# Projecting queries and keys with one 512-column matmul for both halves of the input, in a three-block transformer kernel on one core

## What is computed

```python
# layer 0 of attention (odd_mixer): 16 heads of 64
z = h @ w_in                       # queries, keys, values, and 8 forget gates
y_c = forgetting_attention(...)    # heads 0 to 7, "fox"
y_d = moba_attention(...)          # heads 8 to 15, with a relative bias, "moba"
# layer 1 of attention (second_block)
proj = xn @ w_in                   # queries, keys, values of both kinds
sb_out = stick_breaking_attention(...)      # 8 heads, "stick"
diff_out = differential_attention(...)      # 4 heads with two maps each, "diff"
```

## Time and profile before

| | us |
|---|---|
| median of three executions | 933.09 |
| the profiled execution, its own time | 936.74 |
| its span, first to last instruction | 935.0 |
| TensorE busy in the span | 916.9 |
| VectorE busy | 667.6 |
| ScalarE busy | 552.3 |
| attention steps, layer 0 | about 288 to 379 |
| attention steps, layer 1 | about 594 to 690 |

### The profile page before, as it was taken

The page is one execution under the profiler, slowest core; times in us unless marked ns, Lnnn a source line. Parts: engine busy times, 40 slices in busy tenths (PEclk is TensorE's granted clock), DMA queues, the critical chain, the costliest instruction groups (busy, mean ns, idle before and its releaser), DMA issues.

```text
span 935.0 us, 19813 instructions
## 1 busy us (share of the span) xinstructions
PE 916.9 (98%) x6898; PEld 865.6 (93%) x6898; DVE 667.6 (71%) x1296; ACT 552.3 (59%) x938; POOL 173.5 (19%) x94
## 2 busy tenths in 40 slices
PE   8999999999999999999999999999999999999996
PEld 7999888889998999988888999989999999999996
DVE  6886887786547665788778755787468877785566
ACT  7356776664435556576676545466557666664453
POOL 2320544420000002044443000000203444410000
PEclk9999999999999999999999999999999999999998
DMA  7557765567533544466556653444335655566521
GB/s 276 173 178 218 241 203 184 190 213 263 168 135 106 165 137 136 138 223 204 193 186 213 218 177 135 137 158 136 117 104 186 198 184 180 189 216 205 176 92 46
DMA packets 46329, 163.51 MB, mean 175 GB/s; under 512 B 5010, under 2 KB 9618, under 8 KB 46277
## 3 DMA queue, kind: packets, MB, share of 16 engines
q1 hardware_dynamic: 41704, 158.19, 51.4%
q10 hardware_dynamic: 4573, 4.62, 1.8%
HBM read 161.71 MB, written 3.44 MB: 177 GB/s over the span
## 4 chain that ended last, share of the span: by engine, by line
PE 84%; DVE 6%; issue 5%; ACT 2%; DMA 1%; POOL 1%; SPq 0%; DVEq 0%; ACTq 0%; POOLq 0%
PE psum L1349 17%; PE psum L1370 17%; PE psum L1371 16%; PE psum L1372 16%; PE psum L1350 8%; DVE wl L872 2%; PE psum L1481 1%; PE psum L1483 1%; PE psum L1484 1%; PE psum L1591 1%; DMA raw<-in_even_in 1%; PE psum L1566 1%; ACT wh L534 1%; PE psum L1554 1%; ACT work L712 0%
## 5 line engine op out<-in xcount | busy, mean ns | idle before, releaser
L534 ACT ACTIVATE wh<-raw 128x1024 fp32r<-128x1024 f32 (+2 forms) x270 | 301.1, 1118 | 166.3 <-PE psum L1372 155.0
L872 DVE TENSOR_TENSOR wl<-raw,wh 128x1024 fp32r<-128x1024 f32 (+2 forms) x204 | 272.3, 1339 | 83.7 <-ACT wh L534 83.2
L475 POOL TENSOR_TENSOR wl<-raw,wh 128x1024 fp32r<-128x1024 f32 x66 | 160.0, 2425 | 620.6 <-ACT wh L534 620.6
L1349 PE MATMUL psum<-xs,wh 128*128 128x512 f32 x704 | 247.1, 397 | 0.3 <-POOL wl L475 0.3
L1370 PE MATMUL psum<-xs,wh 128*128 128x256 f32 x800 | 229.7, 287 | 4.3 <-DVE wl L872 2.6
L1371 PE MATMUL psum<-xs,wh 128*128 128x256 f32 x800 | 226.2, 283 | 0.0
L1372 PE MATMUL psum<-xs,wl 128*128 128x256 f32 x800 | 226.2, 283 | 0.0
L1350 PE MATMUL psum<-xs,wl 128*128 128x256 f32 x704 | 196.4, 279 | 0.0
L1370 PE MATMUL psum<-ys,wh 128*128 128x256 f32 x672 | 190.9, 284 | 0.1
L1371 PE MATMUL psum<-ys,wh 128*128 128x256 f32 x672 | 190.1, 283 | 0.0
L1372 PE MATMUL psum<-ys,wl 128*128 128x256 f32 x672 | 190.1, 283 | 0.0
(11 more groups left out here) (212 smaller groups left out, 1008.7 us busy)
## 6 DMA issues: line engine op xcount, KB each, us to landing
raw<-in_up SPq DMA_DIRECT2D x132, 512.0 KB, 3.3
raw<-in_down SPq DMA_DIRECT2D x48, 704.0 KB, 4.3
raw<-in_qkv SPq DMA_DIRECT2D x48, 512.0 KB, 3.3
raw<-in_even_in SPq DMA_DIRECT2D x16, 512.0 KB, 4.0
raw<-in_out SPq DMA_DIRECT2D x16, 512.0 KB, 3.4
raw<-in_ple SPq DMA_DIRECT2D x8, 640.0 KB, 3.9
raw<-in_even_out SPq DMA_DIRECT2D x8, 512.0 KB, 3.3
toeplitz_dram<-table_dram ACTq DMA_DIRECT2D x1, 2048.0 KB
```

Source lines behind the costliest of these rows:

```text
L475: nc.gpsimd.tensor_tensor(low, raw[:, s, 0:tiles * P], high.bitcast(f32), ALU.subtract)\
L534: nc.scalar.activation(split_weights(q, s, tiles * P)[0], raw[:, s, 0:tiles * P], ACT.Copy).then_inc(hi_ready, 1)
L872: nc.vector.tensor_tensor(low, raw[:, s, 0:tiles * P], high.bitcast(f32), ALU.subtract).then_inc(lo_ready[s], 1)
L1349: nc.tensor.matmul(bank, wh[:, s, w], inputs(t), start=first, stop=False)
```

## The change

Query and key units of both attention layers, but for units 0 and 1, become wide units. For each of them ScalarE gets a copy of the first half of the bank into `qkv` (`copy_high`), and VectorE adds the second half and that copy into the first half of the bank, waits for that sum, and then scales as before. In a layer these are 14 units, 28 in all.

```diff
+        def kept_at(u):
+            return u - 1 if u % 6 > 3 else u
+
+        def in_halves(u):
+
+            return u >= 2 and not is_value(u)
...
+        projected = sem("projected")
...
+                def copy_high(u):
+                    if not in_halves(u):
+                        return
+                    act.wait_ge(units_done, base[name] * RING + u + 1)
+                    nc.scalar.activation(qkv[:, kept_at(u), :], qkv_bank(u), ACT.Copy).then_inc(projected, 1)
...
+                    if j < PAIRS:
+                        copy_high(3 * j)
                     if 0 <= j - 1 < PAIRS and not late:
                         softmax_exp(j - 1)
...
                     if j < PAIRS:
+                        copy_high(3 * j + 1)
                         round_next(3 * j + 1)
                         if layer == 0 and j == 0:
                             gate_logs()
+                        copy_high(3 * j + 2)
                         round_next(3 * j + 2)
...
-                    at = u - 1 if u % 6 > 3 else u
+                    at = kept_at(u)
+                    if in_halves(u):
+
+                        dve.wait_ge(projected, (2 * PAIRS - 2) * layer + sum(in_halves(v) for v in range(u)) + 1)
+                        steps(nc.vector.tensor_tensor(qkv_bank(u), psum[:, bank_use(u) % QKV_BANKS, SEQ:2 * SEQ], qkv[:, at, :], ALU.add))
 
                     nc.vector.tensor_tensor(qkv[:, at, :], qkv_bank(u), rstd[:, :], ALU.mult).then_inc(bank_read, 1 + PAIRS if final else 1)
...
-            def wide_unit(q, s, inputs, tiles, start=True, stop=True, ready=None, read=None):
-
-
-                bank = proj[:, s, :]
+            def wide_unit(q, s, inputs, tiles, start=True, stop=True, ready=None, read=None, bank=None):
+
+
+                bank = proj[:, s if bank is None else bank, :]
...
-                        unit(q0 + u // RING, u % RING, qkv_bank(u), from_xs, ALL).then_inc(units_done, 1)
+                        wide_unit(q0 + u // RING, u % RING, both_xs, ALL, bank=bank_use(u) % QKV_BANKS).then_inc(units_done, 1)
```

## The result

The changed kernel takes 944.68 us (median of 4 runs, 942.85 to 946.41); the kernel before, run beside it on the same chip, takes 933.35 us (4 runs). The ratio is 1.0111 with a 95% interval of 1.0091 to 1.0132: slower by 8.5 to 12.3 us. It had been forecast slower by 6.6 us. The profiled execution has an own time of 944.67 us and a span of 942.9 us.

A forecast was written before the change was run, and what follows sets the result against it. TensorE's matmuls were taken as the bound in both attention stretches. Waits less the wide-tile gain gave +1.7 us in layer 0 and +4.9 in layer 1, +6.6 on the median 933.1: 939.7 us, range 935.5 to 942.5.

The forecast's parts named there:

- scores of pair 1: TensorE waits for unit 5's read-out, delayed by VectorE's additions: 1.25 us new in layer 0, 0.85 us in layer 1.
- first weighing: Layer 0: the weighing needs the copy of forget sums, now ending at 304.1, while TensorE arrives at 303.7; 0.4 us.
- scores of pair 2: Layer 0: read-out 7 too late, 0.2 us new wait; layer 1: the existing 0.9 us wait for it grows 0.45 us.
- scores of pair 7: Layer 0: scores follow unit 23 with only the turning between and no margin; 0.8 us new wait.
- longer wait before the first turning: Layer 0: gain of units 4 and 5 is lost in the existing 1.4 us wait, which depends on neither; 0.15 us.
- squares: Layer 1: the matmul of squares waits for the output copy, behind VectorE's lateness from the third addition; 0.9 us.
- weighing of pair 2: Layer 1: it waits for `copy_turned`, which stands behind a root waiting for VectorE; 0.25 us.
- softplus of step 5: Layer 1 stick pairs: softplus, behind unit 3j+1's read-out, has 0.65 us margin, used up by copy and addition; 1.1 us wait.
- The second rival: VectorE catches up during the first stalls, so layer 1's later ones don't come: +2.9 us, 936.0 us; chance 0.2.
- I take 0.350 ... 2.2 us: Attention's wide tiles take 0.350 us against 0.360 narrow; 28 units of 8 tiles gain 2.2 us, half in each layer.
- I put the difference on the median: Profiled execution lay 3.65 us above the median, so +6.6 us was added to the median 933.1, giving 939.7 us.
- nothing else is issued: Beyond one ScalarE copy and one VectorE addition per unit: no DMA, no SP or GpSimd change, no other bank.

The follow-up runs named there:

- from_six: Changed kernel with units 4 and 5 of each layer left narrow as before, so scores of pair 1 have no addition ahead; 941.25 us, one execution.
- wide_no_add: Changed kernel without its copies and additions: 28 wide units, the low half of each sum left out of the result; 935.59 us, ratio 1.0004.
- pe_padded: Changed kernel with 392 already satisfied waits on TensorE, two after each of the first seven tiles of the 28 wide units; 941.77 us, ratio 1.0075.
- after_again: The changed kernel run once more, unchanged; 944.44 us, ratio 1.0106 to the kernel before.
- padded: Changed kernel with 224 always satisfied waits at the end of GpSimd's program; 943.61 us, ratio 1.0103.
- moved_picked: Kernel before with nine wide units (seven in layer 0, two in layer 1) and layer 1's middle-stage scalings and reciprocal moved later; 934.56 us, ratio 0.9993.
- before_again: The kernel before the change run once more, unchanged; 934.91 us, ratio 1.0003.
- pool_scale: Changed kernel with scaling of wide units 6 to 22 on GpSimd, VectorE only adding; units 2 to 5 and 23 narrow; 945.28 us, ratio 1.0109.
- before_moved: Kernel before with layer 1's eight middle-stage scalings moved to steps 6 to 9 and the reciprocal to the end of step 2; 933.14 us, ratio 0.9995.

## Why the prediction was wrong where it was

**The stalls: right.** Forecast and measured waits, in us.

| layer 0 | forecast | measured |
|---|---|---|
| scores of pair 1 | 1.25 | 1.09 |
| first weighing | 0.4 | 0.34 |
| scores of pair 2 | 0.2 | none |
| scores of pair 7 | 0.8 | 0.92 |
| longer wait before the first turning | 0.15 | 0.13 |

| layer 1 | forecast | measured |
|---|---|---|
| scores of pair 1 | 0.85 | 0.73 |
| squares | 0.9 | 0.73 |
| scores of pair 2 (0.92 before) | 1.37 | 1.38 |
| weighing of pair 2 | 0.25 | none |
| weighing of pair 3 | 0.8 | 0.71 |
| softplus of step 5 | 1.1 | 1.05 |
| scores between the two softplus waits | 0.4 | 0.27 |
| softplus of step 6 | 1.2 | 1.00 |

Eleven of the thirteen came, each within 0.2 us; the two that did not were small. The new idle time is 2.5 us in layer 0 (2.8 forecast) and 5.1 in layer 1 (6.05). The second rival (later stalls don't come) is wrong: the profile after has them, and from_six has them even without the early ones.

**The gain: too large.** The step "I take 0.350 ... 2.2 us" gave 1.4 to 1.5 us (wide_no_add). Read from the starts there, successive wide tiles in attention lie 0.353 us apart in layer 0 and 0.349 in layer 1, and narrow ones in the kernel before 0.359. So the pace was nearly right, but where TensorE comes to a unit from other work, its first tile takes 0.42 to 0.46 us, wide or narrow, and gives nothing. And in layer 1 of the changed kernel nothing of the gain is left: TensorE's busy time rose by 0.19 us where wide_no_add lost 0.77. Where that 1 us went was not measured. Gain and waits were off in opposite directions, so it is partly luck that the sum of +7.1 stands so near the forecast +6.6.

**The step that failed** is "I put the difference on the median". It held everything outside attention fixed, and "nothing else is issued" covered added instructions only. The change also *removes* 224 matmuls and their weight loads from TensorE's program, and that has a price: loads at the start land 1.4 us later, stores at the end 0.6 to 0.7 us later. The three stages in which the nine late-starting profiles differ from the eight others, with the same code in all (mean us):

| | late | others | difference |
|---|---|---|---|
| start, to the first norm's sum | 19.00 | 18.38 | 0.62 |
| first stage | 72.99 | 71.30 | 1.69 |
| last norm's sum to the end | 37.25 | 36.65 | 0.60 |

pe_padded undoes the late landings and leaves the copies and additions as they are, and it comes to +7.0 us and 941.8 us, within the forecast range (935.5 to 942.5).

The first stage is the largest of the three. In all 17 profiles it hangs on whether GpSimd's split or VectorE's square starts first (the last section has the rows of both cases). Where GpSimd is first, the square takes 2.29 to 2.60 us and TensorE waits 2.35 to 2.67 us (eight profiles, seven of them late-starting); where VectorE is first, the square takes 0.42 or 0.43 us and TensorE waits 0.5 us at most (nine profiles, two of them late-starting). In the changed kernel:

```profile
22.62 2.35 POOL L483 TENSOR_TENSOR wl<-raw,wh 128x1024 fp32r<-128x1024 f32 x1 [4.97 <-ACT wh L542]
22.70 2.55 DVE L995 TENSOR_TENSOR work<-rstd 128x256 f32<-128x256 f32 x1
...
25.92 0.36 PE L1392 MATMUL psum<-xs,wh 128*128 128x256 f32 x1 [2.62 <-DVE work L1000]
```

The wait alone makes the stage about 1.1 us longer (72.16 and 72.29 against 71.1 to 71.4 us). The rest is the granted clock. Stretches of the changed kernel's first stage:

```profile
25.00:27.30 2.30, 1.38 (x12) 1.41 (x13) 2.21 (x5) 0.00 (x0) 0.90 (x3) 1.00 0.01 5
27.30:30.70 3.40, 3.40 (x19) 3.40 (x18) 3.23 (x9) 0.52 (x2) 1.88 (x3) 0.50 0.75 282
30.70:35.00 4.30, 4.30 (x36) 4.25 (x36) 3.15 (x6) 2.57 (x4) 0.00 (x0) 1.00 0.41 143
```

For 3.4 us, after a wait of TensorE of 2.62 us, the granted clock is 0.50, the lower level of 1.2 GHz: 19 matmuls in 3.4 us, where the next 4.3 us hold 36. It costs 1.7 us (73.90 against the 72.16 us of after_again, which has the wait and not the fall). Six of the eight profiles with the wait have this fall behind it, all six late-starting; none of the nine without the wait has it. Why a late start puts GpSimd first is not shown.

In the two sets of runs that hold both kernels, the mean is 944.4 us over 8 executions of the changed kernel and 934.8 over 37 of the kernel before, a difference of 9.6 us. Of the 2.5 us beyond attention, start and end account for about 1.2 by the table, and the first stage, by its wait and the fall, can hold the rest. A profile is one execution, though, so what the timed runs owe to each was not measured apart. Nor does the +7.1 hold for every execution: in padded and pe_padded a fall of 3.4 us in layer 1 adds 1.0 and 1.1 us to attention.

## What to carry to other kernels

An edit that costs "one short instruction per unit" is priced by following, for each wait that costs nothing today, how long its releaser had been done; this gave eleven of thirteen stalls to 0.2 us each, while a mean busy share of 71% said that there was room. Where margins differ, change only the units that have one (nine or seven of 28 here), and try such edits together: two that were harmless alone made a wait of 1.18 us in moved_picked. And when a change makes the bounding engine's program shorter or longer, compare the first start and the distance from the last matmul to the end before pricing its stages: about 1.2 us moved there, and 1.7 more in a stage whose code had not changed.

## What the runs showed of the hardware that I had not expected

**A shorter program for TensorE, a later start.** 31 packets of instructions or 32: loads issued at the same time land 1.4 us later, and stores 0.7 us. 392 waits in the code, 196 more instructions in the profile, cost TensorE nothing that shows (attention 0 at 122.25 against 122.17 us) and took 2.7 us off the time. Between 31 and 32 lies the step in every profile here; the mechanism is not shown.

**Two engines on one path into memory.** In before_again, in the first stage:

```profile
21.32 2.35 POOL L475 TENSOR_TENSOR wl<-raw,wh 128x1024 fp32r<-128x1024 f32 x1 [5.01 <-ACT wh L534]
21.36 2.60 DVE L977 TENSOR_TENSOR work<-rstd 128x256 f32<-128x256 f32 x1
```

and in the first profile of the same kernel:

```profile
21.91 0.42 DVE L977 TENSOR_TENSOR work<-rstd 128x256 f32<-128x256 f32 x1
22.03 2.56 POOL L475 TENSOR_TENSOR wl<-raw,wh 128x1024 fp32r<-128x1024 f32 x1 [5.16 <-ACT wh L534]
```

VectorE's square takes 0.42 us when it starts 0.12 us before GpSimd's split, and 2.60 us when it starts 0.04 us after it; it then ends 0.29 us behind the split, and TensorE waits for it 2.67 us instead of 0.24. The Trainium skill (SBUF — State Buffer, Who interferes with whom) says that a VectorE instruction with both inputs in SBUF and a GpSimd instruction that reads SBUF take the same port, that the first holds it for its whole length, and that the other is blocked. The trace agrees, here and, with the roles exchanged, in pool_scale (2.77 us for a scaling whose median is 0.75). In before_moved the square starts 0.03 us ahead of the split and still takes 0.42 us. A move of 0.1 us decides which of the two it is, and so whether the first stage has a wait after which the clock can fall.
